# All gate and up pairs first, gated operands parked in HBM, and the down product as one Strassen step of seven half products

## The reference

```python
h = rms_norm(x, norm_ffn_g) * (1 + sc2) + sh2
ff = (jax.nn.silu(h @ w_gate) * (h @ w_up)) @ w_down      # w_gate, w_up: 1024 x 2816, w_down: 2816 x 1024
x = x + g2 * ff
...
y_prompt = rms_norm(xp, final_norm_g)
y_sample = rms_norm(xs, final_norm_g)
```

## Time and profile before

| | us |
|---|---|
| median of 3 runs | 1374.81 (1374.2 to 1376.19) |
| profiled execution, span from first to last instruction | 1373.8 |
| TensorE busy | 1343.7 (98%) |
| VectorE busy | 899.8 (66%) |
| ScalarE busy | 455.0 (33%) |
| feed-forward products, from the first Strassen product at 688.87 to the end | 684.9 |

### The profile page before, as it was taken

How to read it: one execution, slowest core, us unless ns; L and a number is a source line. 1 busy time by engine, 2 the same in 40 slices (tenths; PEclk the granted TensorE clock), 3 DMA queues, 4 the chain that set the end, 5 groups by cost and what they waited for, 6 DMA issues and landing times.

```text
span 1373.8 us, 23593 instructions
## 1 busy us (share of the span) xinstructions
PE 1343.7 (98%) x9552; PEld 1276.5 (93%) x9552; DVE 899.8 (66%) x1425; ACT 455.0 (33%) x739; POOL 57.3 (4%) x59
## 2 busy tenths in 40 slices
PE   6999999999999999999999999999999999999997
PEld 4799999999997776799999999999999999999997
DVE  5699988363744577677866565555655565656567
ACT  5622221133202443446632232323232313232223
POOL 0200000000021221100000000000000000000000
PEclk9899999999999999999999999999999999999999
DMA  9345524721214311031121202121121212120103
GB/s 354 128 138 171 151 93 111 273 47 27 81 31 119 104 33 37 1 110 31 32 62 32 61 31 61 31 61 49 43 61 31 76 30 62 46 61 31 62 31 127
DMA packets 112951, 107.13 MB, mean 78 GB/s; under 512 B 9552, under 2 KB 97192, under 8 KB 112128
## 3 DMA queue, kind: packets, MB, share of 16 engines
q1 hardware_dynamic: 110288, 105.09, 25.0%
q10 hardware_dynamic: 2608, 1.28, 0.4%
HBM read 88.93 MB, written 9.88 MB: 72 GB/s over the span
## 4 chain that ended last, share of the span: by engine, by line
PE 91%; DVE 5%; ACT 1%; issue 1%; DMA 1%; POOL 0%; SPq 0%; ACTq 0%; DVEq 0%; POOLq 0%
PE PS L1216 30%; PE PS L773 18%; PE PS L1234 17%; PE PS L1126 4%; PE PS L979 4%; PE PS L1347 3%; PE PS L1106 3%; PE PS L1164 2%; PE PS L867 2%; PE PS L1053 1%; PE PS L1073 1%; PE PS L1007 1%; PE PS L1312 1%; PE PS L827 1%; DVE MX L2248 1%
## 5 line engine op out<-in xcount | busy, mean ns | idle before, releaser
L2400 DVE TENSOR_TENSOR EL<-HALF_W,EH 128x512 fp32r<-128x512 f32 x163 | 112.1, 688 | 122.7 <-ACT EH L1682 121.8
L1682 ACT ACTIVATE EH<-HALF_W 128x512 fp32r<-128x512 f32 x163 | 102.2, 627 | 256.8 <-PE PS L1234 151.3
L2536 DVE SCALAR_TENSOR_TENSOR X<-PS,MOD,X 128x792 f32<-128x792 f32 (+2 forms) x240 | 125.3, 578 | 70.3 <-PE PS L1234 70.3
L1216 PE MATMUL PS<-HBL_T,EH 128*128 128x264 f32 x640 | 169.7, 285 | 0.0
L1216 PE MATMUL PS<-HBH_T,EH 128*128 128x264 f32 x640 | 169.4, 285 | 0.0
L1234 PE MATMUL PS<-AL,EH 128*128 128x264 f32 x640 | 162.7, 285 | 0.0
L1234 PE MATMUL PS<-AH,EH 128*128 128x264 f32 x640 | 162.3, 284 | 0.0
L773 PE MATMUL PS<-HH,WH 128*128 128x352 f32 x432 | 139.8, 324 | 1.6 <-DVE CQ L2115 0.8
L773 PE MATMUL PS<-HL,WH 128*128 128x352 f32 x432 | 139.1, 323 | 0.0
L1216 PE MATMUL PS<-HBH_T,EL 128*128 128x264 f32 x640 | 130.2, 285 | 0.0
L1216 PE MATMUL PS<-HBL_B,EH 128*128 128x264 f32 x480 | 127.2, 285 | 0.0
(11 more groups left out here) (337 smaller groups left out, 2849.9 us busy)
## 6 DMA issues: line engine op xcount, KB each, us to landing
ADA<-in_w_ada SPq DMA_DIRECT2D x22, 1024.0 KB, 5.8
HALF_W<-in_w_gate SPq DMA_DIRECT2D x22, 512.0 KB, 3.8
HALF_W<-in_w_up SPq DMA_DIRECT2D x22, 512.0 KB, 3.9
HALF_W<-in_w_down SPq DMA_DIRECT2D x22, 512.0 KB, 3.7
RAW<-in_w_in SPq DMA_DIRECT2D x20, 512.0 KB, 6.5
x_saved_rows<-X SPq DMA_DIRECT2D x2, 2112.0 KB, 11.7
X<-x_saved_rows SPq DMA_DIRECT2D x4, 1056.0 KB, 6.0
out<-ORW SPq DMA_DIRECT2D x8, 512.0 KB, 2.6
```

The costliest lines, as they stand in the source:

```text
L1216: mm = pe.matmul(PS[:, 2 * s + n, 0:HQ], w, x[:, k, n * HQ:(n + 1) * HQ], start=(first and w is wh and x is xh), stop=(ends and w is wl), ...
L1682: act.activation(dst if len(src.shape) == 2 else dst.rearrange("p (k c) -> p k c", k=2), src, ACT.Copy)\
L2400: dve.tensor_tensor(el, src, eh.bitcast(F32), ALU.subtract).then_inc(entry_lo, 1)
L2536: ins = dve.scalar_tensor_tensor(dst, src, MOD[:, G2 + m, st:st + 1], dst, ALU.mult, ALU.add)
```

## The change

The gate and up products of all pairs now run one after another, with no down between them. Of each pair the gated rows are not split but combined: of the four blocks of gated values (two feature blocks x two halves of the tokens) VectorE makes four differences (T1, T2, T3, T4; T3 takes the place of one block), and SP stores the seven operands of the pair, 128 x 528 each, in a DRAM tensor TS. A fourth weight buffer (RAW3) and a fourth entry (EH3, EL3) are added; a gate or up product is unchanged.

After the last up product the down product is one Strassen step over all 2816 features: seven products (order P5 P1 P6 P7 P3 P2 P4), each over 11 k-steps, one for each pair, 4 blocks m and half of the tokens. For product q and step k SP loads the operand (DTR, 264 KB) and, where needed, a quarter block of w_down (256 KB, into DWR, SW or AW1) into buffers that lie where the operands of gate and up lay; VectorE makes the weight sum, ScalarE the high parts DTH and DWH, VectorE the rests DTL (in the place of DTR) and DWL. A buffer of step k is loaded again when TensorE is through step k of the product before. Products q = 0 and q = 3 are copied out of PSUM by ScalarE (COPY) and added to X by VectorE later, those of q = 1, 2 and 4 are added by VectorE from PSUM (drain); these stand in the engines' orders ahead of step k = 8 (EARLY) of the next product's preparation. Products q = 5 and q = 6 are each made in pieces of 272 and 256 columns, with the seven transposes (turn) between them.

The core of the diff:

```diff
-ENTRIES, PRODUCTS, KEPT_ACT, KEPT_DVE = 18, 22, 7, 15
+PAIRS = NG - 1
+ENTRIES, PRODUCTS, KEPT_ACT, KEPT_DVE, FIRST = 14, 14, 7, 7, 8
+DOWN = ("P5", "P1", "P6", "P7", "P3", "P2", "P4")
+SAVED = ("B11", "T3", "B21", "B22", "T1", "T2", "T4")
+SUMMED = {0: 0, 2: 1, 3: 2, 4: 3}
+EARLY = 8
...
+            def store_pair(i):
+
+                wait_again(sp, t_made, 4 * i + 8)
+                sp.dma_start(saved(i + 1, 0, 4), blocks(UP[:])).then_inc(a_stored[0], 16)
+                sp.dma_start(saved(i + 1, 4, 6), TB[:]).then_inc(a_stored[0], 16)
+                sp.dma_start(saved(i + 1, 6, 7), blocks(SG[:])[:, 2:3, :]).then_inc(a_stored[0], 16)
...
+            sp.wait_ge(product_full, end + PRODUCTS)
+            sp.wait_ge(entry_lo, end + PRODUCTS)
+            for k in range(4, NG):
+                load_down(SW[k], k, 1, 1)
+            load_down(DWR[NG - 1], NG - 1, 1, 0)
+            store_pair(PAIRS - 1)
+            wait_again(sp, a_stored, 48 * PAIRS)
+            load_operand(0, NG - 1, DTR[NG - 1])
+            for q in range(1, 6):
+                for k in range(NG):
+                    wait_down_step(sp, q - 1, k)
+                    load_operand(q, k, DTR[k])
+                    if q == 1:
+                        load_down(AW1[k], k, 0, 0)
+                    if q == 3:
+                        load_down(DWR[k], k, 1, 0)
+                    if q == 4:
+                        sp.wait_ge(down_lo, 2 * (NG * 3 + k + 1))
+                        load_down(AW1[k], k, 0, 1)
...
+            for k in range(NG):
+                wait_down_step(sp, 5, k)
+                load_down(DWR[k], k, 1, 1)
...
-            with pe.Fori(0, NG - 1) as i:
+            with pe.Fori(0, PAIRS) as i:
                 gate(i)
-                down(i)
-                up(19, 8, 15, i)
-            last_down()
+                up(i)
+            for q in range(5):
+                down_product(q)
+            last_products()
...
+            def down_product(q):
+
+                for k in range(NG):
+                    pe.wait_ge(down_lo, 2 * (NG * q + k + 1))
+                    for m in range(4):
+                        if k == 0:
+                            down_slot_free(q, m)
+                        s = DOWN_SLOT[m]
+                        wh, wl = (w[k][:, m * P:(m + 1) * P] for w in (DWH, DWL))
+                        xh, xl = DTH[k], DTL[k]
+                        for w, xs in ((wh, (xh, xl)), (wl, (xh,))):
+                            for n in range(2):
+                                for x in xs:
+                                    mm = pe.matmul(PS[:, 2 * s + n, 0:HQ], w, x[:, n * HQ:(n + 1) * HQ],
...
+            for q in range(5):
+                for k in range(NG):
+                    if k == EARLY and q in (0, 3):
+                        copy_product(q)
+                    operand_hi_down(q + 1, k)
+                    weights_hi_down(q + 1, k)
...
+            def prepare_down(q, k):
+
+                n = NG * q + k
+                if q in SUMMED:
...
+                    dve.tensor_tensor(dst[k][:], a[k][:], b[k][:], op).then_inc(down_sum[0], 1)
+                dve.wait_ge(down_hi, 2 * n + 1)
+                dve.tensor_tensor(DTL[k][:], DTR[k][:], DTH[k][:].bitcast(F32), ALU.subtract).then_inc(down_lo, 1)
+                dve.wait_ge(down_hi, 2 * n + 2)
+                dve.tensor_tensor(DWL[k][:], down_weights(q, k), DWH[k][:].bitcast(F32), ALU.subtract).then_inc(down_lo, 1)
...
+            for q in range(5):
+                for k in range(NG):
+                    if k == EARLY and q not in (0, 3):
+                        drain(q)
+                    prepare_down(q + 1, k)
...
+            for k in range(NG):
+                last_weights_lo(k)
+                if k in (2, 6):
+                    finish_rows(2 + k // 4)
+                if k == EARLY:
+                    drain_part(1, 0)
```

More of the change, by code:

```diff
@@ L1848, in _, with up @@
-            with act.Fori(0, NG - 2) as i:
-                gate(i)
-                down(i)
-                up(False, i)
-            gate(NG - 2)
-            down(NG - 2)
-            up(True, NG - 2)
-            act.wait_ge(a_split, 2 * NG + 2)
-            act.activation(E3H[:].rearrange("p (k c) -> p k c", k=2), down_block(3, 4), ACT.Copy).then_inc(entry_hi, 1)
+                round_weights(9, i)
+            def up(i, first=False, last=False):
+                round_weights(10, i)
+                if not first:
+                    wait_again(act, a_stored, 48 * i)
+                keep_product(part(UP, 0, 0), 2, 16, i)
+                keep_product(part(UP, 1, 1), 3, 17, i)
+                round_weights(11, i)
+                keep_product(part(UP, 0, 1), 2, 18, i)
+                round_weights(12, i)
+                round_weights(13, i)
+                if last:
+                    return
+                for pos in range(3):
+                    round_weights(pos, i + 1)
@@ new lines, in copy_product @@
+            def copy_product(q):
+                for m in range(4):
+                    wait_again(act, down_full, 4 * q + m + 1)
+                    if q == 0 and m == 0:
+                        wait_again(act, a_stored, 48 * PAIRS)
+                    if q == 3 and m == 0:
+                        act.wait_ge(down_lo, 2 * (NG * 2 + 1))
+                    act.activation(COPY[:, m, :].rearrange("p (n c) -> p n c", n=2), slot(DOWN_SLOT[m]), ACT.Copy)\
+                        .then_inc(down_copied[0], 1)
@@ new lines, in _ @@
+            gate(0, True)
+            up(0, True)
+            with act.Fori(1, PAIRS - 1) as i:
+                gate(i)
+                up(i)
+            gate(PAIRS - 1)
+            up(PAIRS - 1, last=True)
+            for k in range(NG):
+                operand_hi_down(0, k)
+                weights_hi_down(0, k)
+            for q in range(5):
+                for k in range(NG):
+                    if k == EARLY and q in (0, 3):
+                        copy_product(q)
+                    operand_hi_down(q + 1, k)
+                    weights_hi_down(q + 1, k)
@@ new lines, in _, with add_early @@
+            gate(0)
+            up(0, first=True)
+            with dve.Fori(1, PAIRS - 1) as i:
+                gate(i)
+                up(i)
+            gate(PAIRS - 1)
+            up(PAIRS - 1, prepare=lambda k: prepare_down(0, k))
+            for k in range(3, NG):
+                prepare_down(0, k)
+            def add_early(m, s):
+                dst = X[:, m, 0:HT].rearrange("p (n c) -> p n c", n=2)
+                return dve.scalar_tensor_tensor(dst, slot(s), MOD[:, G2 + m, 0:1], dst, ALU.mult, ALU.add)
```

710 lines of the change are left out of this document (398 added, 312 removed).

## The result

| | before | after |
|---|---|---|
| median (lowest to highest), us | 1374.51 (1373.98 to 1376.19), 4 runs | 1344.61 (1343.65 to 1345.64), 4 runs |
| profiled execution, span, us | 1373.8 | 1342.6 |
| TensorE busy, us | 1343.7 | 1312.1 |

The ratio is 0.9779, 95% interval 0.9765 to 0.9793: faster by 29.9 us. The forecast was 1345.3 us, with a span of 1344.3.

The account below looks back on a forecast made before the run. TensorE, busy for 98% of 1373.8 us, was taken to bound the kernel. Terms of -31.2, -0.9, +0.5 and +2.1 gave -29.5 us, a span of 1344.3 and, with the median 1.0 above, 1345.3 us; range 1342 to 1353.

Parts of the forecast that it names:

- Matmuls: TensorE's down work: 2112 matmuls (257.3 us) removed, seven products (226.1 us) added, -31.2 us.
- Gate and up without the down: Loop over the pairs: other engines' work and the stores stay hidden by TensorE's own work, 0 us.
- From up to down: Start of the down: VectorE's queue frees the PSUM slot of block m = 3 late, 0 to 1.2 us, taken +0.5.
- The two old waits: Last down of the kernel before: TensorE's waits of 0.5 and 0.4 us go with it, -0.9 us.
- The round trip through HBM: Last pair's operands, stored and loaded again in the first down product: in time, 0 us, bound 3.
- Four seams: Between down products, q = 0 to q = 4: load, sum, rounding, rest and addition stay hidden, 0 us, bound 2 each.
- The fifth seam: Between q = 5 and q = 6: bank-freeing addition waits behind step 8's weight load, +2.1 us, bounds 1.2 and 5.
- The sum: Whole kernel: all terms together -29.5 us, giving a span of 1344.3 us.
- A: Between down products: the seams are not covered, since every step needs a landed load; chance 0.20.
- C: Down seams: loads landing in 9.5 us or more cost 5 us at each of six, gain gone; chance 0.03.

Follow-up runs that it names:

- eight_more_dve: Changed kernel with VectorE's subtraction that makes T2 repeated eight more times in each up: 1378.9 us, ratio 1.0034 to the kernel before.
- drain_at_9: Changed kernel with EARLY = 9, copies and additions one step later in the next down product's preparation: 1346.18 us, ratio 0.9803 to the kernel before.
- drain_at_10: Changed kernel with EARLY = 10, copies and additions two steps later, additions of the copies in one group: 1365.17 us, ratio 0.9935 to the kernel before.
- last_store_twice: Changed kernel with only the last pair's operands stored twice, the second store waiting for the first: 1350.11 us, ratio 0.9827 to the kernel before.
- stores_twice_in_loop: Changed kernel with each pair's three stores made twice, for all pairs but the last: 1344.26 us, ratio 0.9779 to the kernel before.

## Why the prediction was right

Point by point, by its own steps.

- **Matmuls, -31.2 us: held.** Ten pairs at 41.08; five products in 161.9 us including the wait of 0.3, forecast 161.4; the 528 matmuls in pieces about 65 us, forecast 64.7. TensorE's busy time from the first Strassen product on fell by 30.7.
- **Gate and up without the down, 0: held,** and with more room than was said. The loop takes 3.0 us more in VectorE's queue without a wait, and begins to wait at 4.1. The prediction had given only the nearest slack of ScalarE, about 1 us, and none for VectorE.
- **From up to down, +0.5: 0.3,** on the operation it named (L2775).
- **The two old waits, -0.9: they went.** The wait of 0.7 before the last transposes (L2896) stands in their place in the list, but it isn't new: one of 0.6 on the same kind of addition stood in the last down of the kernel before, which the prediction did not list.
- **The round trip through HBM, 0, bound 3: 0 with some 1.7 us to spare,** 0.54 of it on ScalarE's side, the least of the covered seams. The store was issued 6.4 us into the down, as forecast, and SP was through it at 14.0, forecast 13. The bound was for SP there at about 18 (a store of 11.7 us); with the store doubled SP was there at 20.1, TensorE waited 4.3 us, and the clock, which the bound left out, took 2.5 more.
- **Four seams, 0, bound 2 each: 0,** with 2.1 us to spare at the dearest, where 1 was forecast: 1.26 that VectorE had in hand and 0.9 behind its first block. The waits with EARLY = 9 and 10 show that this is what covers the seams. Late by two steps, the five seams cost 4.2 us each, 1.4 of it TensorE's busy time and mostly the clock; the bound of 2, for a landing of 6.5 us, had no clock in it, and no run tried such a landing.
- **The fifth seam, +2.1: 1.7.** Mis-sized mainly by the landing of a 256 KB load, 2.67 us here where 2.9 to 3.2 was taken. The Trainium skill (DMA: Bandwidth & Descriptors, Anatomy of one DMA) has a fixed part of about 2.0 us plus bytes over 436 GB/s, an estimate of 2.6 us for this load and +1.7 for the term. The page gives this for DMAs that GpSimd issues, which the prediction did not say, and these are issued by SP: this one landing agrees, 2.67 us, and so does the shortest landing of the 264 KB loads, 2.6; their median of 2.9 us lies above it.
- **The sum.** 1344.3 of span were forecast, 1342.6 measured. Ahead of the first Strassen product the profiled execution was 1.4 us earlier (687.50 against 688.87), which is within the scatter of the experiments (685.7 to 689.0). From that product to the end it is 655.1 against 684.9 us, -29.8, where -29.5 was forecast, so the errors of the steps together come to 0.3 us; part of that is luck, since the fifth seam (0.4) and the start of the down (0.2) came out shorter than forecast and the matmuls saved a little less (30.7 us of TensorE's busy time, not 31.2). The median lay 2.0 us above the span, forecast 1.0. In the executions on record the device time is 1.8 to 2.2 us above the span for the kernel before and 1.7 to 1.9 for the changed ones, so the profiled execution of the kernel before was about 1 us slower than its median. That does not touch the forecast, which takes 29.5 us from the median before: 29.9 were measured.

Rivals: A (the seams not covered) held against it that at most 180 GB/s are wanted; q = 0 moved 324, with the last weights and the store in it, and still no load came late enough to be waited for before the fifth seam. C (slower, by loads that land late at every step) needed L of 9.5 us at every step; the median was 2.9 and the longest 6.8. There is a nearer way to the same end, which no rival named: VectorE's queue. In eight_more_dve the pairs have 1.8 us more of it than the loop covers, and with the clock the whole gain of 30 us is gone. The prediction let the clock join in from a wait of 4 us on; the runs have it behind waits of 1.8 to 3.8 us too.

What stays open: the 0.8 us of busy time in drain_at_9, and what decides which waits of about 1.7 to 2.5 us cost clock and which don't (next section but one).

## What to carry to other kernels

On a kernel whose critical engine is busy for 98%, count instructions of that engine at their pace, then list for every added step the place where its queue is nearest to being late: the forecast was good because the few places with about 2 us or less to spare were found by name. State for each such place how far its edge is, not only that it is covered: eight more VectorE operations of 0.74 us per pair turned the gain of 30 us into a loss. And price a wait of TensorE not by its length alone: in these runs most waits of 1.8 to 3.8 us cost 1.5 us on top by the clock, and those of 4.3 and 5.0 us 2.4 to 2.5.

## What the hardware showed that was not expected

The Trainium skill (TensorE: Matmul & The Clock Gate, Part 1) has that the clock is at half rate after idling until the array has been busy again; the trace agrees (in drain_at_10 0.52 behind the wait, 1.00 from 1172.2 to 1175.0 us).
- **A store that others queue behind costs more than its own length.** In last_store_twice the second 1.85 MB held SP up for 6.1 us, and one of the loads that were then issued in one bunch took 6.56 us to land; the median of the operand loads is 2.9.
- **The traffic itself was free.** With 154.75 MB by DMA against 107.13 MB before, TensorE waited behind a load of the down only at the fifth seam, and 17 MB more in stores_twice_in_loop moved no time that could be measured.
